# Both norms' reciprocal roots taken on a 128x4 tile with tokens on partitions, spread by turns of a broadcast column and copied by ScalarE, and the compression moved one tile back

## The reference, cut to what matters

```python
def rms_norm(x, g):
    x32 = x.astype(jnp.float32)
    y = x32 * lax.rsqrt(jnp.mean(x32 * x32, axis=-1, keepdims=True) + EPS)
    return (y * g.astype(jnp.float32)).astype(x.dtype)

def hybrid_layer(x, ...):
    h = rms_norm(x, norm1_g)
    z = h @ w_in
    # four branches of z: short convolution, attention (with compressed keys), retention, pooling
    ...
    x = x + merged @ w_o
    h = rms_norm(x, norm2_g)
    u_gate, u_val = jnp.split(h @ w_up, 2, axis=-1)
    return x + (jax.nn.silu(causal_dwconv(u_gate, ffn_conv)) * u_val) @ w_down
```

## Time and profile before

| | |
|---|---|
| Time, median of 3 runs | 2092.7 us (2092.09 to 2094.68) |
| The profiled execution's own time | 2092.94 us |
| Its span, first to last instruction | 2091.2 us |
| PE busy | 2044.3 us, 98% of the span |
| DVE busy | 1216.9 us, 58% |
| ACT busy | 682.9 us, 33% |
| POOL busy | 917.6 us, 44% |
| Mean granted TensorE clock | 0.992 of 2.4 GHz |

### The profile page before, as it was taken

One profiled execution on the slowest core, in us unless ns is written; L12 is line 12 of the kernel. 1 busy time (PEld: TensorE's weight loads), 2 busy tenths in 40 slices (PEclk: granted clock), 3 DMA queues, 4 the chain that ended last, 5 costly groups with the idle time before them and its releaser, 6 DMA issues.

```text
span 2091.2 us, 31895 instructions
## 1 busy us (share of the span) xinstructions
PE 2044.3 (98%) x9764; PEld 1637.6 (78%) x9764; DVE 1216.9 (58%) x1811; ACT 682.9 (33%) x1001; POOL 917.6 (44%) x672
## 2 busy tenths in 40 slices
PE   8999999999999999999999999899999999999997
PEld 6777667888888888888877777678888888888886
DVE  7766866523226888862257677663322278888522
ACT  5255523333232322222233554232323232222222
POOL 3422223444444555545544212335444455555552
PEclk9999999999999999999999999999999999999998
DMA  5311122223222222223233112222222222232333
GB/s 208 96 62 52 62 74 93 81 100 100 93 98 99 93 97 93 100 85 119 91 120 101 51 52 65 88 86 91 98 97 96 100 91 92 99 100 92 102 107 104
DMA packets 57431, 194.88 MB, mean 93 GB/s; under 512 B 7040, under 2 KB 7552, under 8 KB 57216
## 3 DMA queue, kind: packets, MB, share of 16 engines
q1 hardware_dynamic: 52576, 186.17, 26.6%
q10 hardware_dynamic: 4768, 7.61, 1.4%
HBM read 186.67 MB, written 2.10 MB: 90 GB/s over the span
## 4 chain that ended last, share of the span: by engine, by line
PE 87%; DVE 8%; issue 3%; ACT 1%; ACTq 0%; DMA 0%; DVEq 0%; SPq 0%
PE acc L1185 27%; PE acc L1187 26%; PE acc L1186 26%; PE o L1385 2%; PE s L1359 2%; PE t L1367 1%; PE o L1418 1%; PE s L1408 1%; DVE pT L967 1%; DVE pT L964 1%; DVE win_k L775 0%; DVE rk L759 0%; PE s L1268 0%; DMA w_raw<-weights_dram 0%; DVE rstd L748 0%
## 5 line engine op out<-in xcount | busy, mean ns | idle before, releaser
L433 POOL TENSOR_TENSOR w_lo<-w_raw,w_hi 128x512 fp32r<-128x512 f32 x668 | 917.4, 1394 | 1148.5 <-ACT w_hi L455 1132.3
L1185 PE MATMUL acc<-xg_hi,w_hi 128*128 128x512 f32 x1904 | 771.2, 405 | 5.6 <-DVE xg_lo L697 3.0
L1187 PE MATMUL acc<-xg_hi,w_lo 128*128 128x512 f32 x1904 | 744.0, 391 | 0.0
L1186 PE MATMUL acc<-xg_lo,w_hi 128*128 128x512 f32 x1904 | 743.3, 390 | 0.0
L455 ACT ACTIVATE w_hi<-w_raw 128x1024 fp32r<-128x1024 f32 x336 | 355.3, 1057 | 822.9 <-PE acc L1187 777.7
L1185 PEld LDWEIGHTS acc<-xg_hi,w_hi 128*128 128x128 f32 x1904 | 358.4, 188 | 114.9 <-issue 29.0
L1186 PEld LDWEIGHTS acc<-xg_lo,w_hi 128*128 128x128 f32 x1904 | 358.8, 188 | 77.8 <-issue 7.3
L1187 PEld LDWEIGHTS acc<-xg_hi,w_lo 128*128 128x128 f32 x1904 | 358.4, 188 | 76.7
L1062 DVE TENSOR_TENSOR work<-acc,rstd 128x512 f32<-128x512 f32 x64 | 44.1, 689 | 256.2 <-PE acc L1187 256.2
L1186 PE MATMUL acc<-act_lo,w_hi 128*128 128x512 f32 x352 | 136.9, 389 | 0.0
L1185 PE MATMUL acc<-act_hi,w_hi 128*128 128x512 f32 x352 | 136.9, 389 | 0.0
(11 more groups left out here) (207 smaller groups left out, 2237.4 us busy)
## 6 DMA issues: line engine op xcount, KB each, us to landing
w_raw<-weights_dram SPq DMA_DIRECT2D x339, 512.0 KB, 3.3
x<-xT_dram SPq DMA_DIRECT2D x8, 256.0 KB, 6.4
rot<-rq ACTq DMA_DIRECT2D x16, 128.0 KB
rot<-rk ACTq DMA_DIRECT2D x16, 128.0 KB
dec<-decay_dram ACTq DMA_DIRECT2D x8, 256.0 KB, 3.2
out_dram<-x SPq DMA_DIRECT2D x8, 256.0 KB, 2.7
con<-consts_dram SPq DMA_DIRECT2D x1, 1406.0 KB, 11.1
w1k<-w_dram SPq DMA_DIRECT2D x2, 512.0 KB, 8.8
```

Source lines behind the costliest of these rows:

```text
L433: nc.gpsimd.tensor_tensor(w_lo[:, slot, part], w_raw[:, slot, part], w_hi[:, slot, part].bitcast(F32), ALU.subtract).then_inc(lo_ready, 1)
L1185: mm(tile, w_h, right_hi, start=first, stop=False)
L1186: mm(tile, w_h, right_lo, start=False, stop=False)
L1187: return mm(tile, w_l, right_hi, start=False, stop=last)
```

## The change

The change has four parts.

1. Each layer's two norms get the small form. `sum_squares` becomes four products with `ssq` as weights and one column of ones, into 4 columns. ACT takes the root of 128x4 into `root4`, DVE its reciprocal. A new step `spread_root` on PE turns each of the four columns, read as a 128x128 block with step 0, into 128 columns of a PSUM bank. ACT copies that bank to `rstd` (`root_spread`). `spread_root` stands after the second quarter of the tile that follows: tile 3 in the first norm, the second feed-forward tile in the second.
2. `compress()` goes from behind tile 5 to behind tile 6, `kc` and `vc` from behind tile 7 to behind tile 8. The turns of tiles 4 and 5 stay behind tiles 5 and 7. DVE's order follows: `take(6)` now stands ahead of the gelu's argument, `take(7)` ahead of the gelu, and the copies of `kc` and `vc` behind `take(8)` and the rotation of `q1`. ACT's tanh goes one step back.
3. The norm at the end spreads by transposes where it used products.
4. PE's opening products on zeros are 14 where they were 10.

```diff
-S_USES = ["sumsq1", "hid_k", "hid_v", "kc", "vc", "kc_swap"]
+S_USES = ["sumsq1", "spread1", "hid_k", "hid_v", "kc", "vc", "kc_swap"]
...
+        root4 = small[:, 220:220 + QT]
...
-                nc.scalar.activation(rstd[:, :], s_of(use)[:, :], ACT.Sqrt, bias=C("eps", 1),
+                nc.scalar.activation(root4, s_of(use)[:, 0:QT], ACT.Sqrt, bias=C("eps", 1),
                                      scale=1.0 / D).then_inc(root_ready, 1)
+
+            def root_spread(use, L):
+
+                act.wait_ge(s_done, s_use(L, use))
+                nc.scalar.activation(rstd[:, :], s_of(use)[:, :], ACT.Copy).then_inc(rstd_ready, 1)
...
+                    if g == 3:
+                        root_spread("spread1", L)
...
-                    if g == 6:
+                    if g == 7:
                         act.wait_ge(v_made, v_count(L, "arg"))
...
                             root("sumsq2", L)
+                            root_spread("spread2", L)
...
-                def inverse_root(use, n):
+                def inverse_root(n):
+                    use, spread_ = f"sumsq{n + 1}", f"spread{n + 1}"
                     dve.wait_ge(root_ready, 2 * L + (n + 1))
-                    ins = ve.reciprocal(rstd[:, :], rstd[:, :])
-                    s_end(ins, use, wait=True)
+                    s_end(ve.reciprocal(root4, root4), use, wait=True)
+                    alone(dve)
+                    dve.sem_inc(inverse_ready, 1)
+                    dve.wait_ge(rstd_ready, 2 * L + (n + 1))
+                    made["s"] += 1
+                    dve.sem_inc(s_free, 1)
...
-                gelu_arg()
                 t_wait("v_slc")
                 t_end(ve.tensor_copy(v_nat[:, 0, :, :], t_of("v_slc")[:, :].rearrange("p (k n) -> p k n", k=QT)), "v_slc")
+                take(6, qT[:, 0, :])
+                gelu_arg()
+                take(7, qT[:, 1, :])
                 gelu()
-                take(6, qT[:, 0, :])
-                take(7, qT[:, 1, :])
...
+                take(8, qT[:, 2, :])
+                rotate("q1", qT[:, 1, :], "cos_a", "sin_a")
                 s_wait("kc")
...
                 s_end(ins, "vc")
-                take(8, qT[:, 2, :])
-                rotate("q1", qT[:, 1, :], "cos_a", "sin_a")
...
-            for _ in range(10):
+            for _ in range(14):
                 mm(acc[1][:, 0:P], rstd[:, 0:P], rstd[:, 0:P], start=True, stop=True)
...
-                    mm(b[:, :], ones, ssq[:, :], start=True, stop=True).then_inc(s_done, 1)
+                    for t in range(QT):
+                        ins = mm(b[:, t:t + 1], ssq[:, t * P:(t + 1) * P], ones[:, 0:1], start=True, stop=True)
+                    ins.then_inc(s_done, 1)
+
+                def spread_root(use, value):
+                    pe.wait_ge(inverse_ready, value)
+                    b = s_begin(use)
+                    last_wait()
+                    for t in range(QT):
+                        ins = nc.tensor.transpose(b[:, t * P:(t + 1) * P], spread(root4[:, t:t + 1], [[0, P]]), ident)
+                    ins.then_inc(s_done, 1)
...
-                                   norm=("sumsq1", L * 16 + DC, 3) if g == 2 else None)
-                    if g == 5:
+                                   norm=("sumsq1", L * 16 + DC, 3, sum_squares) if g == 2 else
+                                   ("spread1", L * 2 + 1, 1, spread_root) if g == 3 else None)
+                    if g == 6:
                         compress()
-                    if g == 7:
+                    if g == 8:
                         pe.wait_ge(v_made, v_count(L, "hid"))
...
-                               norm=("sumsq2", L * 16 + 2 * DC, 3) if k == 0 else None)
+                               norm=("sumsq2", L * 16 + 2 * DC, 3, sum_squares) if k == 0 else ("spread2", L * 2 + 2, 1, spread_root))
...
-                ins = mm(s_bank[1][:, t * P:(t + 1) * P], spread(rstd[:, t:t + 1], [[0, P]]), ident, start=True, stop=True)
+                ins = nc.tensor.transpose(s_bank[1][:, t * P:(t + 1) * P], spread(rstd[:, t:t + 1], [[0, P]]), ident)
```

More of the change, by code:

```diff
@@ L136 @@
 SEQUENCE = [_e for _slot in SIDE for _e in _slot]
-S_USES = ["sumsq1", "hid_k", "hid_v", "kc", "vc", "kc_swap"]
+S_USES = ["sumsq1", "spread1", "hid_k", "hid_v", "kc", "vc", "kc_swap"]
 S_USES += [_e for _e in SEQUENCE if _e[0] in ("gate", "cmp_keys", "cmp_scores", "scores", "ret_scores", "ret_var", "pool")]
-S_USES += ["sumsq2"]
+S_USES += ["sumsq2", "spread2"]
 T_USES = ["v_slc", "v_win"]
@@ L310, in build @@
         root_ready = sem("root_ready")
+        inverse_ready = sem("inverse_ready")
+        rstd_ready = sem("rstd_ready")
         ssq_zero = sem("ssq_zero")
@@ L808, in _ @@
                 then(ve.memset(kc[:, NCMP:32], 0.0))
-                inverse_root("sumsq1", 0)
+                inverse_root(0)
                 then(ve.tensor_tensor(k_cmp[:, :], k_cmp[:, :], rstd[:, :], ALU.mult))
@@ L1125, in up @@
                     ve.tensor_tensor(lo, t3, hi.bitcast(F32), ALU.subtract).then_inc(act_ready, 1)
-                inverse_root("sumsq2", 1)
+                inverse_root(1)
                 assert made == {"s": len(S_USES), "t": len(T_USES), "v": len(V_MADE)}
@@ L1229, in projection @@
                         if norm and q == norm[2]:
-                            sum_squares(*norm[:2])
+                            norm[3](*norm[:2])
                 def s_begin(name):
```

## The result

| | before | after |
|---|---|---|
| Time, median (runs) | 2093.11 us (4) | 2081.39 us (4: 2080.68 to 2083.42) |
| Ratio, 95% interval | | 0.9945, 0.9928 to 0.9962 |
| The profiled execution | 2092.94 us, span 2091.2 | 2083.42 us, span 2081.6 |
| Mean granted clock in it | 0.992 | 0.995 |

The change makes the kernel 0.55% faster, 11.7 us, where I had said 0.25% and 5.3. The profiled execution of after is the slowest of its four; the spans of the two profiled ones differ by 9.6.

What follows compares the result with a forecast made beforehand. PE was taken to work nearly without pause, its largest touched wait being 7.0 us for `win_v`. Terms -7.1 - 0.3 - 1.1 + 0.4 + 1.8 + 0.4 + 0.6 = -5.3 gave a median of 2087.4 us, range 2084.8 to 2090.2.

Steps and rivals of the forecast that it cites:

- The hole: PE's idle stretch before the compression, waiting for `win_v` in each layer; moving the compression closes it whole, -7.1 us.
- the turn: Four turns beside the first layer's compression, slow at the lower clock; without the pause they save 0.3 us once.
- the two returns: Compression, turn and `kc` stand apart, so each layer has two more returns to the matmul stream: +0.4 us in all.
- The small root as cover: After the first norm DVE starts some 1.8 us earlier; counted as nothing, only as cover for later steps.
- The spread: Four spreads on PE behind the norms, 0.45 us each with four turns overlapping: +1.8 us, without waiting for the root.
- The sums: New sums of squares on PE in four norms, 0.1 us dearer each than the old ones-product: +0.4 us.
- The halved row: For the sums: the 0.22 us spacing at the kernel's end, lower clock, taken as 0.11 at the higher clock.
- The two bounds: For the sums in the norms: 0.9 us dearer each, 3.6 in all, or 0.4 cheaper each, 1.6 in all.
- DVE's order: Five copies between the takes of tiles 8 and 9 delay the take of tile 10 by 0.3 us per layer: +0.6.
- The end: Spread in the kernel's last norm, four turns instead of 8 instructions, on the path: -1.1 us.
- ACT's order and the opening: ACT's copy ahead of the weights' high part in the second norm, and four more opening products: both cost nothing.
- more is gained: Rival: cheaper sums in the norms give 2085.4 us, or a compression that follows the clock 2084.6; chance 0.10.

Runs made afterwards that it cites:

- e1: Kernel before with the compression one tile later and DVE's and ACT's order that belongs to it, norms, end and opening as before; 2089.95 us, ratio 0.9981.
- e3: Kernel before with only the spread at the kernel's end made by transposes in place of products; 2092.61 us, ratio 0.9998.
- e4: Changed kernel with 10 opening products on zeros instead of 14; 2082.40 us, ratio 0.9948 against the kernel before.
- e8: Changed kernel with the second norm's root made in the old way; 2081.37 us, ratio 0.9945 against the kernel before.
- e12: Changed kernel with `ret_end` of the first retention head one slot later, that head's gate wrong; 2074.39 us, ratio 0.9911 against the kernel before.
- e11: Kernel before with `ret_end` of the first retention head one slot later, that head's gate wrong; 2081.82 us, ratio 0.9948.
- e2: Kernel before with the small roots and their spreads in both norms, compression, end and opening as before; 2085.54 us, ratio 0.9963.
- e10: Kernel before with twelve increments of a spare semaphore on PE behind each norm's ones-product; 2095.28 us, ratio 1.0011.

## Why the prediction was right in direction and too small

- **The hole, the turn, the two returns** (-7.1, -0.3, +0.4): right. From the hole's start to the second matmul behind it the first layer spent 49.09 - 45.44 + 4.49 + 0.08 = 8.2 us, and spends 0.44 for the turn (47.40 - 46.50 less two spacings) and 4.0 for the compression: -3.8, the second -3.6. With 0.1 a layer for `kc` standing apart that is -7.2, where I had -7.0. The compression didn't follow the clock, so it was right that the sum counts no gain there.
- **The small root as cover:** right that it frees 1.6 to 1.8 us (`k_cmp` is scaled 1.6 us earlier, counted from the start of the stream), wrong about what it covers. I put its lead at nothing and wrote that the hole closes by the move alone. e1 shows that without the lead the takes of tiles 4 and 5 are late, 2.7 us in all. The -7.1 came true because the lead was there, and not for the reason that I gave. I had looked only at tiles 8 to 10.
- **The spread, +1.8:** right, 0.43 each, no wait for the root. The clock behind the spreads and turns stayed at 1.00 (33 to 36, 46 to 50 and 1059 to 1063 us). The Trainium skill, "TensorE: Matmul & The Clock Gate", Part 4 (PE-mode transpose), gives about 275 ns for one 128x128 turn, and four of them one by one would be 1.1 us, an estimate; the trace, with 0.43 for four, does not agree.
- **The sums, +0.4:** 0.05 each in the first norms and the same in the second, so at most 0.2. The halved row was the right one to take. The two bounds leave out the return of 0.09: with it they are 1.0 dearer and 0.3 cheaper.
- **DVE's order, +0.6:** this step failed in a small way. I took the take of tile 8 as barely late; DVE waits 0.51 before it and 0.18 before that of tile 9, so the copies were covered and the take of tile 10 does not slip. e1 has the same rows with the old roots, so the order and not the root makes that.
- **The end, -1.1:** 0.95 by e3, and 0.4 more in the profiled execution through the clock, which is not the change's.
- **ACT's order and the opening:** nothing, as said (e4 and e8; the group of weights behind ACT's copy waits for nothing new).
- **What failed is that the sum holds nothing outside the stages that the change edits.** All edits together, by these rows, are -6.6 (-7.2, +1.7, +0.2 and -1.35 with the clock at the end), and by e12 against e11, less the 0.7 above, -6.7, where I had -5.3. That alone would have been inside my range. The rest (4.0 in the profiled pair, 5.0 by the runs) comes from the retention heads. My list of rivals had "more is gained" only by products that get cheaper; none had that DVE's instructions could shift against POOL's where the change touches neither. The row for it, PE's largest wait of all, 12.6 us, stood at the top of the view that I read first.
- **The range's lower end,** 2084.8, would have held e2 and not the changed kernel. The medians differ by 2.1 us more than the two profiled spans; that after's profiled execution is the slowest of four is in the result, and its mean clock is 0.995 against 0.997 in the two quickest. Of those no trace is kept, but e8's execution, 4.0 us quicker than after's, shows where such a difference lies: 1.8 in the start, 1.65 behind the first layer's pause for `pr`, 0.7 in the second norms.

**Open:** what the 0.36 us are. Shown is that they follow neither bank, semaphore nor PE's count, that instructions without work on DVE move them, and that both layers, which run the same loop body, have them at the same instruction. That it is the supply of instructions to DVE fits, and is only argued. Where they stand in the changed kernel I have not found; that no filler was put into that kernel leaves this side untested. That POOL makes the 1.77 is better founded: in the fourteen kernels with `ret_end` at its old place, in both layers, the operation takes 1.76 or 1.77 wherever POOL starts 0.05 to 0.08 ahead of it (six kernels), and 0.74 or 0.75 wherever it starts 0.29 or 0.30 behind (eight); in e11, the kernel before with the operation moved clear of POOL's work, it takes 0.74.

## What to carry to other kernels

Before summing an edit's price, go through the largest waits of the whole span and ask for each how little it would take to tip it: where two engines start within 0.3 us of each other on work that slows one of them, any edit upstream can win or lose a microsecond and more, and the pause's clock on top. An edit's worth is best measured with such a race taken out of both kernels (here 7.4 instead of 11.7 us, and 6.7 once the delay that the race had magnified is taken off too), and taking it out may be worth as much as the edit itself. What follows a pause by way of the clock can differ behind the same wait (6.58 and 5.22 us in the two layers of the kernel before), so a pair of traces shows the wait's change and not what it is worth; for that, take the mean over many. Where an engine gets a lead that "covers" something, take the lead away in an experiment to learn what it covers.

## What the runs showed of the hardware

- A delay of 0.36 us at one instruction of DVE, the same in both turns of the loop, moves to another instruction when 3 empty instructions are put 230 us ahead of it, and goes out of sight with 2 or 6. With it out of the way the kernel before gained 1.9, 3.7 and 3.1 us, the fillers' own cost taken off.
- A 128x512 operation of DVE takes 0.74 when it starts 0.29 ahead of POOL's two 128x512 operations and 1.77 when it starts 0.08 behind them.
- 64 products of 62 columns took 3.79 us at a mean granted clock of 0.63 (before: 1.00 up to 50.0, then 0.52) and of 1.00 (after) alike; eight with one column took 1.87 at the lower and 1.05 at the full clock.
- Behind a pause of PE of 3.9 us the granted clock fell in all twelve cases and the same work took 5.0 to 6.6 us, behind 2.5 us it fell in ten of sixteen (5.2 to 5.3 us, and 3.6 in the other six), and behind 0.5 or none in no case (3.6).
- Twelve increments of a semaphore on PE's queue cost nothing inside an unbroken stream of matmuls, and 1.3 us (0.11 each) right behind a wait of PE (e10).
